# A pick of the product-key layer as one gather of 16 KB rows instead of two gathers of 8 KB rows

## The reference

```
qry   = rms_norm(h) @ w_query                        # 8 heads, two halves of 128
s     = scores of both halves against 128 sub-keys   # top 16 of each, then top 16 of 16 x 16 sums
idx   = i0 * 128 + i1                                # one of 16384 experts; 8 heads x 16 = 128 a token
u     = expert_down[idx]                             # rows of 2048
act   = gelu(sum(xb * u))
vv    = expert_up[idx]                               # rows of 2048
h     = h + sum over 128 of (gate * act * vv)
```

## Time and profile before

| | |
|---|---|
| Time, median of 3 runs | 3204.49 us (3202.22 to 3206.82) |
| The profiled execution | 3205.98 us, span 3204.2 us |
| PE busy | 2913.3 us, 91% of the span |
| DVE, ACT, POOL busy | 1240.0, 549.9, 697.3 us |
| Moved by DMA | 1208.77 MB, 377 GB/s over the span |
| q0 (gathers) | 74064 packets, 537.41 MB |
| q1 (loads) | 66656 packets, 670.13 MB |
| Longest line of the chain | transfers of `down` rows, 31% |

### The profile page before, as it was taken

The page is one execution under the profiler, slowest core; times in us unless marked ns, Lnnn a source line. Parts: engine busy times, 40 slices in busy tenths (PEclk is TensorE's granted clock), DMA queues, the critical chain, the costliest instruction groups (busy, mean ns, idle before and its releaser), DMA issues.

```text
span 3204.2 us, 24141 instructions
## 1 busy us (share of the span) xinstructions
PE 2913.3 (91%) x7992; PEld 1293.4 (40%) x7992; DVE 1240.0 (39%) x1930; ACT 549.9 (17%) x1309; POOL 697.3 (22%) x657
## 2 busy tenths in 40 slices
PE   8999999899989999897687888887889999999999
PEld 3444444344444444343233333333344553333344
DVE  1101004635454443445766755554632232322220
ACT  1111001112121110111313211221222121000010
POOL 0000001323223222322534433334500010110000
PEclk9999999999999999998899888988989999999999
DMA  9877887999999999999999999999977779999972
GB/s 389 294 277 288 302 347 305 414 422 421 421 421 420 421 422 422 421 421 419 406 422 409 421 422 421 421 421 420 409 298 275 250 309 425 429 428 429 429 318 79
DMA packets 140819, 1208.77 MB, mean 377 GB/s; under 512 B 15616, under 2 KB 18224, under 8 KB 20144
## 3 DMA queue, kind: packets, MB, share of 16 engines
q1 hardware_dynamic: 66656, 670.13, 52.2%
q0 software_dynamic: 74064, 537.41, 40.5%
HBM read 1205.38 MB, written 2.10 MB: 377 GB/s over the span
## 4 chain that ended last, share of the span: by engine, by line
PE 48%; DMA 40%; DVE 4%; issue 4%; DVEq 2%; ACT 1%; POOL 1%; SPq 0%; ACTq 0%; POOLq 0%
DMA W<-in_peer_expert_down,big 31%; PE bank L993 13%; DMA W<-experts 7%; PE bank L1559 6%; PE bank L983 6%; PE bank L1651 5%; PE bank L1169 4%; PE bank L1721 3%; PE bank L1060 3%; DVE W L2704 2%; DVEq L2481 2%; PE bank L1633 2%; PE bank L1675 1%; DMA W<-units_of 1%; DMA XT<-in_peer_expert_up,big 1%
## 5 line engine op out<-in xcount | busy, mean ns | idle before, releaser
L2704 DVE CUSTOM_DVE_ANT_0 W<-W,big 128x2048 f32<-128x2048 f32 x256 | 586.5, 2291 | 748.9 <-DMA W<-in_peer_expert_down,big 745.1
L909 POOL DMA_INDIRECT W<-in_peer_expert_down,big x256 | 342.9, 1340 | 1230.2 <-DVE small L2704 669.8
L1559 PE MATMUL bank<-XT,big 128*128 128x512 f32 x488 | 302.9, 779 | 194.6 <-ACT big L2006 158.8
L993 PE MATMUL bank<-W,XT 128*128 128x512 f32 x672 | 294.8, 596 | 0.0
L1559 PE MATMUL bank<-XS,big 128*128 128x512 f32 x536 | 250.6, 611 | 30.5 <-ACT big L2006 16.1
L1998 ACT ACTIVATE small<-small 128x1 f32<-128x1 f32 x256 | 52.0, 203 | 1262.4 <-DVE small L2704 1258.2
L1559 PEld LDWEIGHTS bank<-XT,big 128*128 128x128 f32 x488 | 118.6, 252 | 367.9 <-issue 264.8
L1559 PE MATMUL bank<-W,big 128*128 128x512 f32 x512 | 237.2, 607 | 20.4 <-ACT big L2006 16.9
L1651 PE MATMUL bank<-W,XS 128*64 128x512 f32 x1024 | 224.9, 593 | 5.2 <-DMA W<-experts 5.0
L983 PE MATMUL bank<-W,XT 128*128 128x512 f32 x480 | 213.2, 602 | 10.7 <-DMA W<-units_of 10.3
L1169 PE MATMUL bank<-W,XT 128*128 128x512 f32 x464 | 204.0, 592 | 1.7 <-ACT big L1807 1.7
(11 more groups left out here) (370 smaller groups left out, 2569.0 us busy)
## 6 DMA issues: line engine op xcount, KB each, us to landing
W<-units_of SPq DMA_DIRECT2D x102, 2048.0 KB
W<-experts SPq DMA_DIRECT2D x68, 2048.0 KB, 17.1
W<-units_of SPq DMA_DIRECT2D x128, 1024.0 KB, 10.4
big<-experts SPq DMA_DIRECT2D x32, 2048.0 KB, 12.4
W<-in_w_in SPq DMA_DIRECT2D x32, 1024.0 KB
W<-in_w_ret_branch SPq DMA_DIRECT2D x16, 1024.0 KB
W<-in_w_out SPq DMA_DIRECT2D x16, 1024.0 KB
W<-in_w_peer_query SPq DMA_DIRECT2D x16, 1024.0 KB
```

The source lines that it names most:

```text
L909: pool.indirect_dma_start(down_row(n), None, down_t, row).then_inc(down_in[n % DOWN_ROWS], 16)
L993: mm = pe.matmul(out, lhs(k), slot(i)[:, k, :], start=first and k == 0, stop=last and k == ks - 1)
L1559: mm = pe.matmul(bank[4 * (n // P) + c][:, :], DIAG[:, m % 4, :], up_row(n)[:, c * CH:(c + 1) * CH], start=n % P == 0, stop=n % P == P - 2)
L2704: dve.tensor_tensor_reduce(out=down_row(n), in0=down_row(n), in1=HN[n // P], scale=1.0, scalar=0.0, op0=ALU.mult, op1=ALU.add, accum_out=d ...
```

## The change

`kernel()` lays the two tables side by side, so that an expert is one row of 4096 numbers (`expert_rows`). A pick is one gather of 128 rows of 16 KB, issued when the place is free, that is when the sum of the pick before in this place has ended; `down` is its first half and `up` its second. The places are `W[:, 2]`, `W[:, 3]`, `XS`, and for tile 1 a fourth, which is `XT[:, 1]` together with the first half slot of `W` (for this `XT` and `W` become one tensor `XW`). From tile 0's `in2` units on, weights therefore use three half slots, the first of them the second quarter of the lower `W`. The first two whole units after the picks change slots, and the second waits for the sum of the last pick that used the fourth place (252).

```diff
+        if half and i >= SECOND:
+            s = 1 + (i - SECOND) % (SLOTS - 1)
...
+        if WHOLE_AGAIN <= i < WHOLE_AGAIN + 2:
+            s = 1 - s
...
-def rows_of_up():
+def rows_of_picks():
     rows, seen = [], {}
     for n in range(PICKS):
-        spare = [3] if 12 <= n < P else [4] if n >= P else []
-        ring = [0, 1, 2] + spare
-        b = min(ring, key=lambda b: seen.get(b, (-1, 0))[0])
+        b = min(range(3 if n < P else 4), key=lambda b: seen.get(b, (-1, 0))[0])
...
+LAST_FOURTH = max(n for n in range(PICKS) if ROWS[n][0] == 3)
...
+        def both_rows(n):
+
+            b = ROWS[n][0]
+            return (W[:, 2, :], W[:, 3, :], XSf, XW[:, D:3 * D])[b]
+
         def down_row(n):
-            b = n % DOWN_ROWS
-            return W[:, 2 + b // 2, (b % 2) * D:(b % 2 + 1) * D]
+            return both_rows(n)[:, 0:D]
         def up_row(n):
-            b = UP_ROWS[n][0]
-            return (W[:, 3, D:2 * D], XS[:, 0, :], XS[:, 1, :], XT[:, 0, :], XT[:, 1, :])[b]
+            return both_rows(n)[:, D:2 * D]
...
-            for i in range(INDEX["query", 1, 0], INDEX["in2", 0, 0, 4]):
+            for i in range(INDEX["query", 1, 0], INDEX["in2", 0, 0, 3]):
                 load(i)
...
             for i in range(WHOLE_AGAIN, INDEX["in2", 1, 1, 0]):
+                if i == WHOLE_AGAIN + 1:
+                    sp.wait_ge(added, PE_COUNT[LAST_FOURTH] + 1)
                 load(i)
...
-                if n >= DOWN_ROWS:
-                    pool.wait_ge(dotted, n - DOWN_ROWS + 1)
-                pool.sem_inc(gathers, 1)
-                pool.indirect_dma_start(down_row(n), None, down_t, row).then_inc(down_in[n % DOWN_ROWS], 16)
-                b, earlier, _ = UP_ROWS[n]
+                b, earlier, _ = ROWS[n]
                 if earlier in BY_DVE:
                     pool.wait_ge(added_dve, DVE_COUNT[earlier] + 1)
                 elif earlier is not None:
                     pool.wait_ge(added, PE_COUNT[earlier] + 1)
-                elif b >= 3:
-                    pool.wait_ge(w_used, INDEX[("query", 1, 15) if b == 4 else ("query", 0, 3, 3)] + 1)
+                elif b == 3:
+                    pool.wait_ge(w_used, INDEX["query", 1, 15] + 1)
                 pool.sem_inc(gathers, 1)
-                pool.indirect_dma_start(up_row(n), None, up_t, row).then_inc(up_in[b], 16)
+                pool.indirect_dma_start(both_rows(n), None, expert_rows, row).then_inc(rows_in[b], 16)
...
-                    dve.wait_ge(down_in[n % DOWN_ROWS], 16 * (n // DOWN_ROWS + 1))
+                    dve.wait_ge(rows_in[ROWS[n][0]], 16 * ROWS[n][2])
...
+    laid.update(units_of_8=laid_units(inputs, WHOLE), units_of_4=laid_units(inputs, HALF), experts=by_expert(inputs),
+                expert_rows=np.concatenate([inputs["peer_expert_down"][0], inputs["peer_expert_up"][0]], 1))
```

More of the change, by code:

```diff
@@ L34 @@
 W2_F, W2_RX, W2_RG = 3072, 3080, 4104
-DOWN_ROWS = 3
 def order_of_units():
@@ L66 @@
 INDEX = {key: i for i, key in enumerate(ORDER)}
-HALVES, WHOLE_AGAIN = INDEX["query", 0, 1, 0], INDEX["in2", 1, 0, 0]
+HALVES, SECOND, WHOLE_AGAIN = INDEX["query", 0, 1, 0], INDEX["in2", 0, 0, 0], INDEX["in2", 1, 0, 0]
 UG = INDEX["ple", 0]
@@ L89, in places_of_units @@
         half = HALVES <= i < WHOLE_AGAIN
-        s = (i - HALVES - len(EARLY) * (i > INDEX[EARLY[0]]) if half else i - WHOLE_AGAIN if i >= WHOLE_AGAIN else i) % SLOTS
+        if half and i >= SECOND:
+            s = 1 + (i - SECOND) % (SLOTS - 1)
+        elif half:
+            s = (i - HALVES - len(EARLY) * (i > INDEX[EARLY[0]])) % SLOTS
+        else:
+            s = (i - WHOLE_AGAIN if i >= WHOLE_AGAIN else i) % SLOTS
+        if WHOLE_AGAIN <= i < WHOLE_AGAIN + 2:
+            s = 1 - s
         lo, hi = (2048 * s, 2048 * (s + 1)) if half else (UNIT * s, UNIT * (s + 1))
@@ L115, in rows_of_up @@
     return rows
-UP_ROWS = rows_of_up()
+ROWS = rows_of_picks()
+LAST_FOURTH = max(n for n in range(PICKS) if ROWS[n][0] == 3)
 GROUPS = [(0, 0, 1), (0, 1, 1)] + [(g // 4, 2 * (g % 4), 2) for g in range(1, 8)]
@@ L381, in steps_beside_picks, with two_blocks @@
     return pe, act, dve, fifth, ticks
-def two_blocks(nc, A, consts, gains, turned_x, turned_keys, units_of_8, units_of_4, experts, out):
+def two_blocks(nc, A, consts, gains, turned_x, turned_keys, units_of_8, units_of_4, experts, expert_rows, out):
     f32, u32 = mybir.dt.float32, mybir.dt.uint32
@@ L400, in two_blocks @@
         H = sb("H", [P, T2, D])
-        XT = sb("XT", [P, T2, D])
+        XW = sb("XW", [P, T2 * D + SLOTS * UNIT])
+        XT = XW[:, 0:T2 * D].rearrange("p (t n) -> p t n", t=T2)
         XS = sb("XS", [P, T2, D])
-        W = sb("W", [P, SLOTS, UNIT])
+        W = XW[:, T2 * D:].rearrange("p (s n) -> p s n", s=SLOTS)
         big = sb("big", [P, 19456])
@@ L574, in two_blocks @@
             sem(n) for n in ("best_ready", "gate_exp", "idx_ready", "gate_ready"))
-        down_in = [sem(f"down_in{b}") for b in range(DOWN_ROWS)]
-        up_in = [sem(f"up_in{b}") for b in range(5)]
+        rows_in = [sem(f"rows_in{b}") for b in range(4)]
         gathers = sem("gathers")
@@ L814, in _ @@
             sp.dma_start(GROW, A["final_norm"].unsqueeze(0).to_broadcast([P, D])).then_inc(grow_loaded, 16)
-            for i in range(INDEX["in2", 0, 0, 4], WHOLE_AGAIN):
+            for i in range(INDEX["in2", 0, 0, 3], WHOLE_AGAIN):
                 load(i)
@@ L1554, in _ @@
                     m = PE_COUNT[n]
-                    b, _, count = UP_ROWS[n]
-                    pe.wait_ge(up_in[b], 16 * count)
+                    b, _, count = ROWS[n]
+                    pe.wait_ge(rows_in[b], 16 * count)
                     pe.wait_ge(diag_ready, m + 1)
@@ L2475, in add_weighed @@
             def add_weighed(n):
-                b, _, count = UP_ROWS[n]
+                b, _, count = ROWS[n]
                 h, j = H[:, n // P, :], n % TOPK
                 dve.wait_ge(weight_ready, DVE_COUNT[n] + 1)
-                dve.wait_ge(up_in[b], 16 * count)
+                dve.wait_ge(rows_in[b], 16 * count)
                 dve.drain()
@@ L3005 @@
 INPUTS = ["x", "attn_norm", "w_in", "attn_sinks", "w_attn_branch", "w_ret_branch", "w_out", "ffn_norm",
-          "w_peer_query", "peer_sub_keys", "peer_expert_down", "peer_expert_up", "final_norm", "p_2",
+          "w_peer_query", "peer_sub_keys", "final_norm", "p_2",
           "mix_norm_2", "w_in_2", "b_forget_2", "q_norm_2", "k_norm_2", "conv_w_2", "conv_b_2",
@@ L3025 @@
     laid = {"gains": columns_of_gains(inputs), "turned_x": x.reshape(P, T2, D), "turned_keys": keys.reshape(P, 16, P)}
-    laid.update(units_of_8=laid_units(inputs, WHOLE), units_of_4=laid_units(inputs, HALF), experts=by_expert(inputs))
+    laid.update(units_of_8=laid_units(inputs, WHOLE), units_of_4=laid_units(inputs, HALF), experts=by_expert(inputs),
+                expert_rows=np.concatenate([inputs["peer_expert_down"][0], inputs["peer_expert_up"][0]], 1))
     for name, a in laid.items():
@@ L3033 @@
     two_blocks(nc, aps, consts, aps["gains"], aps["turned_x"], aps["turned_keys"], aps["units_of_8"],
-               aps["units_of_4"], aps["experts"], out)
+               aps["units_of_4"], aps["experts"], aps["expert_rows"], out)
     r = run_bass_kernel_spmd(nc, [arrays], core_ids=[0])
```

1 line of the change is left out of this document (removed).

## The result

The kernel after takes 3247.94 us (median of 4 runs, 3241.54 to 3255.25) against 3203.65 for the kernel before in the same comparison (3202.22 to 3206.82): ratio 1.0131, 95% interval 1.0116 to 1.0146. It is 1.3% slower. The prediction was 3190 us, with a range up to 3216 and a chance of 0.20 for slower.

A forecast was written before the change was run, and what follows sets the result against it. Picks were taken as bound by DMA bytes, with PE last in a third of tile 0. Terms -16.2 + 5 + 1 - 5 = -15.2 us took the profiled 3205.98 to 3190.8, the median to 3189.3, rounded to 3190; range 3170 to 3216.

The forecast's parts named there:

- Longer hold of a place: Places held until the pick's sum: +5 us in tile 0 (0 to +39), 0 in tile 1.
- Rival A: Tile 0: three places run dry while GpSimd waits for the sum of n-3; +39 instead of +5, 3224 us; chance 0.19.
- five passages: Tile 0, near 820, 1040, 1185, 1343 and 1425 us: PE-last stretches end with up to 2 MB less; 4.9 us each, 25 us.
- The sign named for A: DMA share falls below 0.95 in 950 to 990 and 1485 to 1590 us, in tile 0.
- Size: All picks: 16 KB rows move at 428 GB/s, not 421 to 422; -19.5 us, -16.2 without picks where PE is last.
- Rival B: Gathers: a 16 KB row moves as two 8 KB packets, so -16.2 becomes 0; 3208 us; chance 0.08.
- D: Gathers alone on the engines rise from 412 to 428 GB/s, fewer gaps left; another 11 us faster, 3178 us; chance 0.13.
- Start: Pick 0's dot waits for 2 MB instead of 1, up to 5 us later; +1 us taken (0 to +5).
- Tile 1: Four places at 4.0 us a pick against picks every 6.2 us, so the hold costs 0 us (-5 to +5).
- End: Last picks: 255 asked for behind 254's 2 MB, with packets equal in size to the weights'; -5 us (-10 to +3).
- Packet turns: Tile 0: gathers get two thirds of the engines while both queues hold work, but engines stay full; 0 us.
- rival C: Weights come late by the turns of packets: 2.5 us in each of six stretches, 15 us; 3205 us; chance 0.08.

The follow-up runs named there:

- other execution of the same program: Kernel after with the first 2 MB weight unit issued when one dot is left instead of two, the same program up to pick 253: 3243.72 us, 1.0109.
- hold-alone run: Kernel before, but in tile 0 the down rows of pick n are asked for only when the sum of n - 3 has ended: 3236.87 us, 1.0099.
- tile-1-alone run: Tile 0's picks as in the kernel before, tile 1's as in the kernel after (one gather, four places): 3207.91 us, 1.0001.
- fourth place from pick 114: Kernel after, with the fourth place used from pick 114 on instead of 128: 3237.92 us, 1.0098.
- loads one dot later: Kernel after, with the first 2 MB weight unit behind the picks issued when one dot is left instead of two: 3243.72 us, 1.0109.
- two waits alone: Kernel before; in tile 0 down gathers wait for the sum of n - 3 and a dot waits for both down and up rows: 3279.14 us, 1.0218.
- control: Kernel before, with each 1 MB weight unit of tile 0's picks loaded as two column halves in 4 KB packets: 3233.73 us, 1.0085.

## Why the prediction was wrong

**The step that failed is "Longer hold of a place", tile 0: +5 us taken, +37 measured** (the lag at pick 127, +50 in the other execution of the same program; the lag contains whatever the larger rows gained there). Rival A's mechanism and place were right, and its chance of 0.19 was too small. That its high end, +39, is near +37 is partly luck: it has 14 us in the stretches in which gathers are alone, where the lag rose by 30 (9 and 21), and 25 at five passages, where the rest of the 37 is 7. Three things were wrong in the working.

First, the loop was priced from a clean spot: 15.2 and 18.2 us, 16.0 in the mean, 5.3 a pick. In the kernel after, for picks 114 to 127, the timelines give in the mean 11.0 us from issue to dot, 9.1 from dot to the end of the sum, and 0.8 to the next issue in that place: 20.9 us, and 20.9 / 3 = 7.0 is the interval at which these picks come. That last is no proof by itself, since three places that are refilled at once always give it; the proof that the loop binds is the DMA share of 0.89 and the empty slices at 1522 to 1526. Of the 4.9 us missing, 3.1 are in issue to dot: the estimate let a gather have the engines alone, while two are in flight; those issued between 1520 and 1530 us landed 9.0 and 10.5 us after their issue. Another 1.2 are in the hold: the clean spot had a sum at the full clock (3.67 us), while TensorE's granted clock is 0.81 in this stretch (0.83 before, so that was readable), with sums of 5.40 and 6.66 us where others take 3.60. The last 0.6 are before the issue.

Second, the later start of the dot was counted once, at pick 0. It stands in every turn of the loop. By itself it costs 8 us, and the hold 32; together 70. The prediction had one of the two and took a mean against a mean ("where picks come every 9.1 us nothing shows"). But in shared stretches the loop is longer too: for picks 61 to 104 it is 12.7 us from issue to dot, 13.0 to the end of the sum and 0.8 to the next issue, 26.6 us, a third of it 8.9. Tile 0 lost 8 us by pick 48, for which the sum had no room; the share of 0.78 from 600 to 640 us is one place of it.

Third, "Against it: the first 12 picks have only three `up` places in the kernel before too" compared unlike things. There `down` places come free at the dot, so `down` runs ahead; the hold-alone run has just that taken away, and costs 32 us.

The sign named for A came in part: the share is 0.82 and 0.92 in the stretches that answer to the two named, but 0.97 and 0.98 over tile 0, not below 0.95 over most of it. Holes in a few stretches were enough.

**Size, -16.2.** The signs named for it came in part: 37200 packets, and 424 to 427 GB/s in slices that are full, but over the picks of tile 1 only 422 against 420. Tile 1's part (9.7 us by the working) shows as 1 to 8 us, and by the tile-1-alone run it nets to nothing with the end. In tile 0 a rate is worth nothing while engines run dry. Rival B is out. So is D: where gathers are alone and the engines full (the fourth place from pick 114) they move 410 GB/s, against 412 before.

**Start, +1.** 0.0 us at the sum of pick 0: right.

**Tile 1, 0.** Right: the same kernel in tile 1 alone is level.

**End, -5.** Wrong in sign: +11 from pick 248 to 255. The working had 254's 2 MB ahead of the weight units and only 255's beside them. But GpSimd issues 254 when it has waited 8.6 us for a PE sum, 0.8 us before the units: its 2 MB share the engines with 4 MB from the start. The rule of turns that was used there is not at fault; the order of issue was. The run with the loads one dot later takes the 17 us of pick 254 away.

**Packet turns, 0.** Weights are in the chain of tile 0 now, with pieces of 14 to 19 us, so rival C's mechanism is there. PE's waits for weights beside the picks (lines 1063 and 1172) are small, 17 us in five entries of the list, and not all of them lie on the end. How much is the turns' doing wasn't isolated. The premise of the term, two thirds of the engines for gathers, holds for some us at a time; from 645 to 705 us they had 49.3%.

In sum, in the profiled execution: +37 in tile 0, -1 in tile 1, +11 at the end, +2 behind the picks: +49, against the -15 forecast. What is shown is that the order of the places makes the loss in tile 0 (the two waits alone, the fourth place from pick 114, tile 1 alone). How the single gather of 16 KB rows wins back 38 of the 80 us is open.

## What to carry to other kernels

Merging two transfers also merges their waits: the place is held until the last reader, and the first reader starts at the last byte. Draw the loop of one place (free, issue, land, first use, last use), fill it with durations from the stretch in which the transfers are alone, at the clock that is granted there and with as many in flight as there will be, and compare it with places times the interval. Two small delays in one loop don't add: 32 and 8 us made 70. A buffer moved from weights to gathers was dearer here (54 us) than what it bought (14).

## What the runs showed of the hardware

While both queues hold work, they move the same number of packets, for three pairs of sizes. In the kernel before, with 8 KB on both, it is 290 against 288 from 690 to 700 us. In the control with 4 KB weight packets, 690 to 700 us, and in the kernel after, 695 to 700 us:
```profile
q0 software_dynamic: 384, 2.76, 66.5%
q1 hardware_dynamic: 384, 1.43, 35.7%
```
```profile
q0 software_dynamic: 90, 1.47, 69.3%
q1 hardware_dynamic: 91, 0.66, 31.7%
```
Equal counts, and two thirds of the engines for the packets that are twice as large. It lasts only as long as both queues have something to move: in the 60 us from 645 on the counts are 1 to 2 in both kernels, and each queue has half of the engines. The Trainium skill (DMA: Bandwidth & Descriptors, "Queues, rings and completion order") tells of turns of a packet too. These counts agree with it; whether single packets alternate, or several at a time, they don't show. The rate by packet size at a full DMA (share 1.00 to 1.02): 415 GB/s with 4 KB weights beside 8 KB gathers (680 to 780 us of the control), 421 with both at 8 KB, 425 with 16 KB gathers beside 8 KB weights. So larger rows are worth 1% only. That one gather of 16 KB rows beats two of 8 KB by 38 us at the same hold was not expected. In tile 0 it is 71.4 - 37.4 = 34 us, 0.27 us a pick (71.4 - 50.3 = 21 us, 0.16, with the other execution). The Trainium skill (SBUF — State Buffer, "The DMA setup-cost knee") gives about 2 us for a transfer's fixed part. These runs show at most a seventh of it a pick; that other transfers lie over the rest is an argument, which no run tests.
